# A hybrid decoder step on one Trainium2 core: odd expert slabs loaded through GpSimd's queue, even ones through SyncE's

## What is computed

```python
def _swiglu(h, wg, wu, wd):
    return (jax.nn.silu(h @ wg) * (h @ wu)) @ wd

def _moe(h, router, wg, wu, wd):
    logits = jnp.einsum('btd,de->bte', h, router).astype(jnp.float32)
    top_v, top_i = lax.top_k(logits, TOP_K)
    probs = jax.nn.softmax(top_v, axis=-1)
    combine = jnp.sum(jax.nn.one_hot(top_i, N_EXPERTS, dtype=jnp.float32) * probs[..., None], axis=-2)
    y = jnp.zeros(h.shape[:-1] + (wd.shape[-1],), h.dtype)
    for e in range(N_EXPERTS):
        y = y + combine[..., e:e + 1].astype(h.dtype) * _swiglu(h, wg[e], wu[e], wd[e])
    return y
```

## Time and profile before

| | |
|---|---|
| median of 3 runs | 1570.3 us (1568.53 to 1574.8) |
| the profiled execution's own time | 1576.22 us |
| its span | 1574.1 us, granted TensorE clock 0.985 of full speed |
| PE busy | 1527.1 us (97%) |
| DVE, ACT, POOL busy | 629.0 us (40%), 322.8 us (21%), 56.2 us (4%) |
| DMA | 299.71 MB, mean 190 GB/s over the span |
| expert stage, from routing (about 1160 us) to the last down product (1560 us) | 400 us |

### The profile page before, as it was taken

The page is one execution under the profiler, slowest core; times in us unless marked ns, Lnnn a source line. Parts: engine busy times, 40 slices in busy tenths (PEclk is TensorE's granted clock), DMA queues, the critical chain, the costliest instruction groups (busy, mean ns, idle before and its releaser), DMA issues.

```text
span 1574.1 us, 39435 instructions
## 1 busy us (share of the span) xinstructions
PE 1527.1 (97%) x17569; PEld 1257.5 (80%) x17569; DVE 629.0 (40%) x1450; ACT 322.8 (21%) x764; POOL 56.2 (4%) x68
## 2 busy tenths in 40 slices
PE   8999999999999999999999999999989999999986
PEld 6887776887779999987887777877768787788765
DVE  5133346744145656543235267643232221222212
ACT  1432113222112212133331123221120000000001
POOL 1000010110000000000000000200010000000000
PEclk9999999999999999999999999999999999999998
DMA  8333435212544444336525353125878999999993
GB/s 337 107 108 115 168 117 140 84 35 79 210 142 157 151 149 157 108 142 222 201 81 192 122 138 103 43 65 164 340 263 312 329 318 349 320 332 349 340 398 128
DMA packets 64324, 299.71 MB, mean 190 GB/s; under 512 B 21839, under 2 KB 23567, under 8 KB 37663
## 3 DMA queue, kind: packets, MB, share of 16 engines
q1 hardware_dynamic: 50392, 268.10, 47.3%
q0 software_dynamic: 2944, 18.09, 3.1%
q10 hardware_dynamic: 10823, 11.05, 2.6%
HBM read 277.93 MB, written 19.28 MB: 189 GB/s over the span
## 4 chain that ended last, share of the span: by engine, by line
PE 93%; DVE 2%; issue 2%; DMA 1%; ACT 1%; SPq 0%; DVEq 0%; ACTq 0%
PE ps L996 16%; PE ps L1576 15%; PE ps L1725 14%; PE ps L1452 11%; PE ps L1658 7%; PE ps L1459 6%; PE ps L1515 4%; PE ps L988 4%; PE ps L1308 2%; PE ps L1609 2%; DMA ring<-in_mix 1%; PE ps L1006 1%; PE ps L1284 1%; PE ps L1044 1%; PE ps L1356 0%
## 5 line engine op out<-in xcount | busy, mean ns | idle before, releaser
L996 PE MATMUL ps<-xn,ring 128*128 128x288 f32 x928 | 237.8, 413 | 0.0
L996 PEld LDWEIGHTS ps<-xn,ring 128*128 128x128 f32 x928 | 175.5, 192 | 50.6 <-issue 2.8
L1452 PE MATMUL ps<-xn,ring 128*128 128x288 f32 x768 | 203.0, 412 | 0.8 <-ACT gate L2034 0.4
L1452 PEld LDWEIGHTS ps<-xn,ring 128*128 128x128 f32 x768 | 142.1, 190 | 48.9 <-issue 11.7
L1576 PE MATMUL ps<-y_ml,arena 128*64 128x96 f32 (+5 forms) x3584 | 143.9, 244 | 15.0 <-issue 14.9
L1576 PEld LDWEIGHTS ps<-y_ml,arena 128*64 128x64 f32 x3584 | 140.8, 142 | 19.9 <-issue 19.8
L1725 PE MATMUL ps<-arena 128*128 128x144 f32 x1028 | 133.4, 285 | 0.0
L1725 PEld LDWEIGHTS ps<-arena 128*128 128x128 f32 x1028 | 129.3, 189 | 0.0
L1658 PE MATMUL ps<-arena,mixed 128*32 128x256 f32 x2024 | 111.5, 379 | 0.5 <-issue 0.5
L1658 PEld LDWEIGHTS ps<-arena,mixed 128*32 128x32 f32 x2024 | 65.7, 110 | 43.1 <-issue 1.2
L2815 DVE TENSOR_TENSOR mixed<-ps,mixed 128x96 f32<-128x96 f32 (+5 forms) x88 | 21.7, 247 | 190.1 <-PE ps L1576 181.4
(11 more groups left out here) (506 smaller groups left out, 1845.4 us busy)
## 6 DMA issues: line engine op xcount, KB each, us to landing
arena<-in_egu SPq DMA_DIRECT2D x56, 1024.0 KB, 6.2
ring<-in_mix SPq DMA_DIRECT2D x46, 1024.0 KB, 6.2
arena<-in_edown SPq DMA_DIRECT2D x40, 1024.0 KB, 6.1
ring<-in_mix SPq DMA_DIRECT2D x48, 768.0 KB, 4.3
ring<-in_egu SPq DMA_DIRECT2D x32, 1024.0 KB, 6.7
ring<-in_gu SPq DMA_DIRECT2D x14, 1024.0 KB, 4.8
arena<-in_gu SPq DMA_DIRECT2D x8, 1024.0 KB, 5.7
arena<-in_C POOLq DMA_DIRECT2D x2, 2048.0 KB, 8.1
```

Source lines behind the costliest of these rows:

```text
L996: last = mm(bank[:, 0:T], ring[:, s, w0:w0 + P], (xn if n else xgain)[:, k, :], start=(k == 0), stop=(k == KT - 1))
L1452: last = mm(ps[:, bank, 0:T], ring[:, s, P * k:P * k + P], xn[:, k, :], start=(k == 0), stop=(k == KT - 1))
```

## The change

Even slabs of passes 1 to 7 stay on SP's queue, odd ones move to POOL's. On each queue a slab is issued only when that queue's last slab has landed. On SP this holds in passes 1 to 6, as before; in the loop SP waits for `e_used` alone. On POOL it holds in the loop too. The odd slabs share one new semaphore, `e_odd`, which PE waits for in passes 1 to 7. `IN_FLIGHT` goes away.

```diff
-IN_FLIGHT = 2
@@
+        def expert_slab(e, k):
+
+            if k < FT:
+                src, width = a["egu"][bass.ds(e * FT + k, 1)], SLOT
+            else:
+                width = D * len(DOWN[k - FT])
+                src = a["edown"][bass.ds(e * DSL + (k - FT), 1), :, 0:width]
+            return eslab(k)[:, 0:width], src.rearrange("a p n -> p (a n)")
@@
+        e_odd = sig("expert_odd_slab_loaded")
+
+        def odd_loaded(p, k):
+            return p * (16 * (ETURNS // 2)) + (16 * ((k + 1) // 2) - 16 * (ETURNS // 2))
@@ SP
                 def expert(p, e):
-                    for k in range(ETURNS):
+                    for k in range(0, ETURNS, 2):
                         sp.wait_ge(e_used.sem, p * ETURNS + (k + 1 - ETURNS))
                         if isinstance(p, int):
-                            j = (k - IN_FLIGHT) % ETURNS
-                            sp.wait_ge(e_ld[j].sem, p * 16 + (16 if k >= IN_FLIGHT else 0) + expert_loads(j))
...
-                        sp.dma_start(eslab(k)[:, 0:width], src.rearrange("a p n -> p (a n)")).then_inc(e_ld[k].sem, 16)
+                            j = k - 2 if k > 0 else ETURNS - 1
+                            sp.wait_ge(e_ld[j].sem, p * 16 + (16 if k > 0 else 0) + expert_loads(j))
+                        sp.dma_start(*expert_slab(e, k)).then_inc(e_ld[k].sem, 16)
@@ PE
-                pe.wait_ge(e_ld[k].sem, p * 16 + 16 + expert_loads(k))
+                if k % 2 == 0 or isinstance(p, int) and p == 0:
+                    pe.wait_ge(e_ld[k].sem, p * 16 + 16 + expert_loads(k))
+                else:
+                    pe.wait_ge(e_odd.sem, odd_loaded(p, k))
                 return eslab(k)
@@ POOL, after the six indirect DMAs
+            def expert(p, e):
+                for k in range(1, ETURNS, 2):
+                    pool.wait_ge(e_used.sem, p * ETURNS + (k + 1 - ETURNS))
+                    if k > 1 or not isinstance(p, int) or p > 1:
+                        pool.wait_ge(e_odd.sem, odd_loaded(p, k) - 16)
+                    pool.dma_start(*expert_slab(e, k)).then_inc(e_odd.sem, 16)
+
+            for p in range(1, FIXED):
+                expert(p, pool.value_load(plan[0:1, p:p + 1], min_val=0, max_val=NE - 1))
+            pool.wait_ge(*extra_ok(0))
+            npass = pool.value_load(plan[0:1, PLAN_N - 1:PLAN_N], min_val=1, max_val=1 + MAXEXTRA)
+            with pool.Fori(0, npass) as i:
+                expert(i + FIXED, pool.value_load(plan[0:1, bass.ds(i + FIXED, 1)], min_val=0, max_val=NE - 1))
```

## The result

| | before | after |
|---|---|---|
| median | 1570.6 us (4 runs, 1568.5 to 1574.8) | 1595.0 us (4 runs, 1592.7 to 1595.0) |
| ratio, 95% interval | | 1.0149 (1.013 to 1.0168) |
| the profiled execution's own time, its span | 1576.22, 1574.1 us | 1592.74, 1590.7 us |

The change costs 24.4 us. The two profiled executions lie only 16.5 us apart, since that of before was 5.6 us over its median and that of after 2.2 us under its own.

What follows compares the result with a forecast made beforehand. It took the kernel as bound by PE's matmuls; POOL's chain, 56 slabs at 7.5 us from 1178.4, ends at 1598.4, 41.0 us after 1557.4. So 1570.3 + 41 = 1611 us, range 1561 to 1667.

Steps and rivals of the forecast that it cites:

- SP ... Its even slabs keep their rule: SP's loads in the expert stage: even slabs wait for landings as before, while SP loses 8 of 17 issues a pass.
- this alone gives nothing: SP's fewer issues in the expert stage: nothing waited for SP's issuing time, so no gain or loss.
- c = 5.4 + 1.4 + 0.7 = 7.5 us: POOL's cycle per odd slab: lone load 5.4, busy engines and issue after a landing 1.4, sharing between queues 0.7 us.
- the threshold of 6.77: POOL's chain of 56 odd slabs: the last is late if a cycle is over 379 / 56 = 6.77 us.
- 1557.4: Time in us at which PE needs slab 15 of pass 7, the very last chance for the odd slabs.
- The chain keeps up: Rival: POOL's cycle stays under 6.77 us, PE goes on as before, no change, 1570 us; chance 0.14.
- Instructions sooner: Rival: PE's 18.2 us of instruction gaps shrink, half of them is -9 us, 1561 us; chance 0.11.
- Instructions later: Rival: a third queue delays PE's instructions at 38 block ends, 1 us each, +38 us, 1608 us; chance 0.23.
- The change doesn't do what it says: Rival: POOL's issue, with addresses from a register, is slow and its cycle grows, again slower; no separate chance.
- POOL's landings of 6.5 to 8 us: Sign on POOL's queue: 56 slabs with this landing time if the forecast is right.
- SP waiting for PE and not for landings: Sign on SP: if the forecast is right, it waits mainly for PE to free buffers (`e_used`).
- lead of 38 us: The lead of the loads, said to melt first, with PE beginning to wait for odd slabs in passes 5 and 6.

Runs made afterwards that it cites:

- e9: The changed kernel with no landing wait on SP and two slabs under way on POOL in all passes; 1579.3 us, 1.0028 to the kernel before.
- e4: The kernel before, all slabs on SP's one queue, with the change's landing waits (slab 0 waits for slab 16, slab 1 for slab 15); 1572.2 us, 1.0014.
- e1: The changed kernel, but SP's slab 0 no longer waits for slab 16 of the last pass; 1599.7 us, 1.0208 to the kernel before.
- e8: The kernel before without the wait for landings, one queue with no limit; 1571.8 us, 1.0018.
- e2: The changed kernel with queues changing sides each pass, each slab of passes 1 to 6 waiting for the one two before; 1602.3 us, 1.0202 to the kernel before.
- e11: The changed kernel with two slabs under way on SP, POOL one (two in pass 7); 1610.5 us, 1.0227 to the kernel before.

## Why the prediction held, and the step that did not

**The sum.** Forecast +41 us, measured +24.4; slower, and in the range. The kind of mechanism was right: a strict chain of loads, one under way, melts the lead of the loads and PE waits for slabs in the last passes. The sign rests on it, and e9 shows it by taking it away. The chain was the wrong one. That the time fell into the range owes something to luck, for two errors worked against each other: POOL's link was priced 0.9 us too long, and SP's chain was left out.

**"SP ... Its even slabs keep their rule", "this alone gives nothing".** This step failed. The chain that was late is SP's, not POOL's. The rule on the even slabs reads the same, but it no longer does the same work. In one queue a link took 53.5 us / 8.5 = 6.29 us, and with nine links to the even chain 5.96 us (e4). Beside POOL's queue each of them takes 6.55 us. I gave the sharing of the DMA engines a price on POOL's side alone. The longer links are on SP's side too, and SP has 63 of the 119 slabs.

**c = 5.4 + 1.4 + 0.7 = 7.5 us.** POOL's link measured 6.58 us over the passes 2 to 6, 0.9 us less. The first term, a lone slab, was about right: the last four of POOL's in e1, with nothing of SP's beside them, landed in 5.1 to 5.4 us. The 1.4 us were taken from SP, 6.3 less 4.9, where they may contain what the second slab in the same queue adds. On POOL, in the change, landing and re-issue came to 5.6 + 0.7 = 6.3 at the median and 6.6 in the mean, so 1.4 and 0.7 together measured 1.2. At 6.58 us the threshold of 6.77 is not reached, and PE never waited for POOL. But pass 7 is in the 56 links too, and there POOL's slabs took up to 11.2 us beside SP's full queue. Over the whole chain c was (1565.4 - 1178.4) / 56 = 6.9 us: the last odd slab landed 8.0 us after 1557.4. By the prediction's own sum POOL's chain cost +8 us, hidden behind the 16.6 us of SP's. That the last pass would stretch the links, because SP has no limit there, stands nowhere in the sum, though "in pass 7 it may queue several even slabs at once" was seen.

**The sum with the right chain.** SP's first load of pass 2 goes out 3.4 us before that of before (1228.9 against 1232.3). Five passes at 59.0 instead of 53.5 us lose 27.6. So that of pass 7 is 24.2 us late. Its cover was 1515.0 - (1499.6 + 7.85) = 7.6 us, by the landing time that it has after. 24.2 - 7.6 = 16.6 us, the growth of the span. This is the measured lateness of slab 0 told in the prediction's terms (links times length, less the lead), all with measured values, and no independent check of them; the lead it used, 379 / 56, was that of the other chain.

**The time of need, 1557.4**, is borne out by e1. There slab 15 of pass 7, the last one late, landed at 1571.3 us, which is 13.9 us after it, and e1's span of 1588.2 us is 14.1 longer than that of before. In the change itself it landed at 1565.4 and held nobody up, since PE was 16.6 us behind by then.

**The rivals.** The chain keeps up: true of POOL's in passes 1 to 6, not of SP's, and so the rival fails. Instructions sooner: the gaps "issue" went from 18.1 to 15.1 us in the change, 3 us against the 22.8 us of late slabs, in which a part of them may simply be hidden. Instructions later: no, the gaps did not grow, and in e9 with the deepest two queues they are 1.5 us more than in e8. The change doesn't do what it says: it does, 56 slabs are on POOL's queue at 0.53 us of issue each.

**The signs to look for.** PE waits for DMA at L1584 and L1669 and 8% of DMA in the chain: seen. POOL's landings of 6.5 to 8 us: 5.6 to 5.9, which is on the side of "the chain keeps up". Its starts 7 to 8 us apart: 6.6. SP waiting for PE and not for landings: the reverse, 302.8 us against 0.9. With the nine waits of PE it says which chain was late. The "lead of 38 us" of the prediction stands in no row and is no term of its sum.

**The two rules cited.** The line of the Trainium skill, "DMA: Bandwidth & Descriptors", section "Anatomy of one DMA — SWDGE (gpsimd) path", gives the estimate of 4.4 us for a slab. POOL's landed in 4.9 us at best and 5.6 at the median in the change, and in 5.1 to 5.4 with nothing of SP's beside them in e1, so the estimate is too short here. The Trainium skill, "DMA: Bandwidth & Descriptors", section "Issuing engines are not separate DMA queues", says that several issuing engines save only the sequencer's time. For the bytes this case agrees: no gain, 345 GB/s on two queues in e9, 344 on one in e8. It does not follow that moving a load costs nothing. With a limit by landings on each, e2 lost 2% to the kernel before, which has the same rule in one queue.

**What stays open** is the way in which SP's link grows by some 0.6 us. SP's re-issue after a landing is unchanged at 0.21 us, so all of it is in the landing. On POOL the re-issue alone takes 0.70 us, 0.5 more than on SP. That two queues are served side by side, so that both slabs land late, agrees with the 10 to 11 us that POOL's slabs took beside SP's full queue in pass 7. It was argued from there, and no run isolates it. A rival stands untested: every second queue of the study is POOL's, with its slower re-issue. No run puts the odd slabs on ACT's queue, so it is not shown whether any second queue with a limit of one would cost this, or only POOL's. Nor is it explained why e2, with 303 GB/s, is as slow as it is.

## What to carry to other kernels

A limit of so many transfers under way is a chain, and what it costs is links times their length, less the lead that the loads have. If it is split over two queues, price both chains, the one that stays as well as the one that is moved, and do not limit either queue to one. Two queues, SP's and POOL's, with one each were 1.5 to 3% slower here than one queue with two. The only pair of queues that kept up was e9's, with no limit on SP and two on POOL; two on each was not run. These two deep queues were worth no more than one. Where a stage is bound by PE with slabs landing some 7 us ahead of need, a faster way of loading has nothing to give and a slower one has only these 7 us. Relieving one of two chains can move the lateness to the other (e1, e11), so test with both relieved before you judge the mechanism.

## What was not expected of the hardware

- Re-issue after a landing: 0.70 us on POOL, 0.21 us on SP, from the issues and landings of the trace of the change, nearly without spread.
- POOL's slab beside one slab of SP's landed sooner than SP's own, in the medians 5.6 to 5.9 against 6.0 to 6.8 us. Beside the slabs that SP had queued for pass 7 three of POOL's took 10.4 to 11.2 us, while SP's landed 2.5 us apart at best.
- One queue with three slabs or any number under way moved 343 to 344 GB/s against 333 with two, and PE's gaps named "issue" grew by only 3 to 4 us over the whole stage.
